# RWKV-7 mixer on Trainium2: key products leave PSUM by ScalarE copies and are masked in SBUF by GpSimd

## What is computed

```python
def rwkv7_scan(r, w, k, v, kk, a):
    def step(state, inp):
        r_t, w_t, k_t, v_t, kk_t, a_t = inp
        sa = jnp.einsum('...vk,...k->...v', state, kk_t)
        state = (state * w_t[..., None, :] - sa[..., :, None] * (kk_t * a_t)[..., None, :]
                 + v_t[..., :, None] * k_t[..., None, :])
        return state, jnp.einsum('...vk,...k->...v', state, r_t)
```

## Time and profile before

| | us |
|---|---|
| runs before, median of 3 | 5032.76 |
| lowest and highest of them | 5032.74, 5043.73 |
| the profiled execution, its own time | 5042.74 |
| its span, first to last instruction | 5041.1 |
| TensorE matmul busy in the span | 3743.1 (74%) |
| VectorE busy | 2186.9 (43%) |
| ScalarE busy | 1087.1 (22%) |
| GpSimd busy | 354.4 (7%) |
| the RWKV mixer, about | 872 to 1800 of the span |

### The profile page before, as it was taken

One profiled execution on the slowest core, in us unless ns is written; L12 is line 12 of the kernel. 1 busy time (PEld: TensorE's weight loads), 2 busy tenths in 40 slices (PEclk: granted clock), 3 DMA queues, 4 the chain that ended last, 5 costly groups with the idle time before them and its releaser, 6 DMA issues. The chain is left out here.

```text
span 5041.1 us, 52437 instructions
## 1 busy us (share of the span) xinstructions
PE 3743.1 (74%) x17350; PEld 2455.9 (49%) x17350; DVE 2186.9 (43%) x4798; ACT 1087.1 (22%) x2308; POOL 354.4 (7%) x437
## 2 busy tenths in 40 slices
PE   8699998677777868888466479923978856629980
PEld 1255554577667768888333234411446633314440
DVE  0212321666666646666378600053125525530007
ACT  0011222333333322222011112210124411102210
POOL 0000000211111100000000011110000000011001
PEclk9899999777777779999777689966989977859995
DMA  7622222300000011011523179953122251229984
GB/s 253 191 59 57 65 66 86 108 27 28 23 27 27 20 50 34 34 38 34 91 101 111 42 276 367 366 195 134 62 70 72 77 82 75 80 81 356 364 308 166
DMA packets 383411, 592.63 MB, mean 118 GB/s; under 512 B 61043, under 2 KB 266907, under 8 KB 383023
## 3 DMA queue, kind: packets, MB, share of 16 engines
q1 hardware_dynamic: 313934, 368.18, 23.9%
q10 hardware_dynamic: 47776, 151.99, 7.7%
q0 software_dynamic: 21584, 71.00, 4.3%
HBM read 466.29 MB, written 124.81 MB: 117 GB/s over the span
## 5 line engine op out<-in xcount | busy, mean ns | idle before, releaser
L373 PE MATMUL inp__bank<-inp__hT,inp__w 128*128 128x512 f32 (+1 forms) x1536 | 559.7, 524 | 10.1 <-DMA inp__w<-in_ab_w_in_dram 8.0
L2142 PE MATMUL moe__bank<-moe__wgu,moe__xT 128*128 128x512 f32 x1024 | 456.4, 599 | 13.2 <-DMA moe__wgu<-in_moe_w_up_dram 11.4
L373 PEld LDWEIGHTS inp__bank<-inp__hT,inp__w 128*128 128x128 f32 x1536 | 290.3, 191 | 272.1 <-issue 251.9
L1775 PE MATMUL close__bank<-close__w_out,close__catT 128*128 128x512 f32 x640 | 312.3, 650 | 101.3 <-DVEq L1916 93.9
L2142 PEld LDWEIGHTS moe__bank<-moe__wgu,moe__xT 128*128 128x128 f32 x1024 | 191.2, 192 | 233.9 <-issue 220.6
L1775 PEld LDWEIGHTS close__bank<-close__w_out,close__catT 128*128 128x128 f32 x640 | 132.5, 211 | 271.0 <-issue 186.4
L2265 DVE TENSOR_TENSOR moe__hid<-moe__sg,moe__bank 128x256 f32<-128x256 f32 x64 | 27.0, 421 | 480.2 <-ACT moe__sg L2204 480.2
L2159 PE MATMUL moe__bank<-moe__wdn,moe__hidT 128*128 128x512 f32 x512 | 230.5, 593 | 2.9 <-ACT moe__hidT L2208 2.9
L2460 PE MATMUL qkv__bank<-qkv__w,qkv__hT 128*128 128x512 f32 x480 | 212.1, 599 | 2.7 <-DVE qkv__hT L2552 2.7
L247 PE MATMUL ada__bank<-ada__w,ada__c_silu 128*2 128x512 f32 x384 | 170.5, 599 | 30.4 <-DMA ada__w<-in_ada_w_dram 27.9
L2035 POOL DMA_INDIRECT scratch_row_tok<-close__tok,close__dest_i x40 | 38.6, 965 | 2182.4 <-DVEq L1704 2170.8
(11 more groups left out here) (404 smaller groups left out, 6581.8 us busy)
## 6 DMA issues: line engine op xcount, KB each, us to landing
moe__wdn<-in_moe_w_down_dram ACTq DMA_DIRECT2D x64, 1024.0 KB, 8.6
moe__wgu<-in_moe_w_gate_dram SPq DMA_DIRECT2D x64, 1024.0 KB
moe__wgu<-in_moe_w_up_dram SPq DMA_DIRECT2D x64, 1024.0 KB
ada__w<-in_ada_w_dram SPq DMA_DIRECT2D x24, 2048.0 KB, 8.0
scratch_y_rows<-moe__y ACTq DMA_DIRECT2D x64, 512.0 KB
scratch_zt<-inp__tb SPq DMA_DIRECT2D x32, 640.0 KB, 5.0
inp__w<-in_ab_w_in_dram POOLq DMA_DIRECT2D x31, 512.0 KB, 4.6
delta__qkv<-scratch_zt SPq DMA_DIRECT2D x20, 768.0 KB, 4.4
```

Source lines behind the costliest of these rows:

```text
L373: mm = nc.tensor.matmul(zbank[j][g][:, 0:n], w[:, j, k, :], hT[:, k, t0:t0 + n], start=k == 0, stop=k == KC - 1)
L1775: mm = pe.matmul(bank[2 + c][:], catT[:, k, :], w_out[:, k, c * 512:(c + 1) * 512], start=k == 0, stop=k == KC - 1)
L2142: mm = pe.matmul(bank[2 + j][:], xT[:, j, k, :], wgu[:, j, k].rearrange("p a n -> p (a n)"), start=k == 0, stop=k == KC - 1)
```

## The change

The four BP instructions stay on VectorE. The four KP evictions leave it: ScalarE copies the four banks unmasked into KP (`copy_kp`), between `place(s+1)` and the eviction of `Un`, and GpSimd multiplies KP by the mask in place (`mask_kp`), between `key(s+3)` and `extra(s+3)`. Two semaphores are new, `kp_ev` (copied) and `kp_r` (masked). TensorE's waits for free banks go to `kp_ev`, and `from_state` waits for `kp_r`; GpSimd's `clear` waits for `kp_r` too, which its own queue has raised by then.

```diff
@@ tensor
                     if i > 0:
-                        pe.wait_ge(prod_ev, 8 * (i - 1) + 8)
+                        pe.wait_ge(kp_ev, 4 * i)
...
                     if have(i + 1):
-                        pe.wait_ge(prod_ev, 8 * (i + 1) + 8)
+                        pe.wait_ge(kp_ev, 4 * (i + 1) + 4)
...
                     if part == 0:
                         pe.wait_ge(hp, i + 1)
+                        pe.wait_ge(kp_r, 4 * i + 4)
@@ scalar
+                def copy_kp(i):
+
+                    if i > 1:
+                        act.wait_ge(pre_mm, i - 1)
+                    for q in (0, 2):
+                        for e in range(2):
+                            act.wait_ge(prod, 8 * i + (4 + q + e + 1))
+                            act.activation(KP[:, i % 2, e, q:q + 2].rearrange("p q a t -> p q (a t)"),
+                                           heads(bank[(6, 7, 2, 3)[2 * e + q // 2]][:], 256), ACT.Copy).then_inc(kp_ev, 1)
...
                     if have(s + 1):
                         place(s + 1)
+                    if have(s + 2):
+                        copy_kp(s + 2)
@@ gpsimd
+                def mask_kp(i):
+                    if i > 1:
+                        pool.wait_ge(x_clear, i - 1)
+                    for q in (0, 2):
+                        for e in range(2):
+                            pool.wait_ge(kp_ev, 4 * i + q + e + 1)
+                            pool.tensor_tensor(KP[:, i % 2, e, q:q + 2].rearrange("p q a t -> p q (a t)"),
+                                               KP[:, i % 2, e, q:q + 2].rearrange("p q a t -> p q (a t)"),
+                                               const(f"mask_k{i % 2}").unsqueeze(1).broadcast_to([P, 2, 256]), ALU.mult).then_inc(kp_r, 1)
...
                         key(s + 3)
+                    if have(s + 2):
+                        mask_kp(s + 2)
+                    if have(s + 3):
                         extra(s + 3)
@@ vector
                 def masked(i, d):
-                    for kind, mask in ((0, f"mask_b{d}"), (1, f"mask_k{d}")):
-                        if kind == 1 and i > 1:
-                            dve.wait_ge(pre_mm, i - 1)
...
+                    for q in (0, 2):
+                        for e in range(2):
+                                dve.wait_ge(prod, 8 * i + (q + e + 1))
+                                dve.tensor_tensor(BP[:, i % 3, e, q:q + 2].rearrange("p q a t -> p q (a t)"),
+                                                  heads(bank[2 + 2 * e + q // 2][:], 256),
+                                                  const(f"mask_b{d}").unsqueeze(1).broadcast_to([P, 2, 256]), ALU.mult).then_inc(prod_ev, 1)
```

More of the change, by code:

```diff
@@ L775, in rwkv_mixer @@
                                 "zeroed", "zero_stored", "rows_scaled"))
-        tr, tr_ev, prod, prod_ev, stacked, n_read, solved, d_placed, y5_mm, y5_ev, x64_mm, x64_ev, y6_mm, y6_ev, gt_mm, gt_ev, x_clear = (
-            ph.sem(n) for n in ("turned", "turned_ev", "products", "products_ev", "stacked", "lanes_read", "solved", "placed", "y5_mm",
+        tr, tr_ev, prod, prod_ev, kp_ev, kp_r, stacked, n_read, solved, d_placed, y5_mm, y5_ev, x64_mm, x64_ev, y6_mm, y6_ev, gt_mm, gt_ev, x_clear = (
+            ph.sem(n) for n in ("turned", "turned_ev", "products", "products_ev", "kp_copied", "kp_masked", "stacked", "lanes_read", "solved", "placed", "y5_mm",
                                 "y5_ev", "x64_mm", "x64_ev", "y6_mm", "y6_ev", "inverse_mm", "inverse_ev", "x_cleared"))
@@ L896, in products @@
                                 if kind == 1 and e == 1 and q % 2 == 0:
-                                    pe.wait_ge(prod_ev, 8 * i + (1 if q == 0 else 3))
+                                    pe.wait_ge(prod_ev, 4 * i + (1 if q == 0 else 3))
                                 b = bank[(2, 3, 4, 5, 6, 7, 2, 3)[4 * kind + 2 * e + q // 2]]
@@ L909, in level5 @@
                     if have(i + 1):
-                        pe.wait_ge(prod_ev, 8 * (i + 1) + 4)
+                        pe.wait_ge(prod_ev, 4 * (i + 1) + 4)
                     for e in range(2):
@@ L1050, in place @@
                         act.activation(XT[quad(b), j, :, quad(b)], solve.Q[quad(b)], ACT.Copy).then_inc(d_placed, 1)
+                def copy_kp(i):
[6 more added lines that the diff above has]
+                                           heads(bank[(6, 7, 2, 3)[2 * e + q // 2]][:], 256), ACT.Copy).then_inc(kp_ev, 1)
                 def stack(i):
-                    act.wait_ge(prod_ev, 8 * i + 4)
+                    act.wait_ge(prod_ev, 4 * i + 4)
                     if i > 0:
@@ L1180, in clear @@
                     pool.wait_ge(b_r, min(i + 3, NT))
+                    pool.wait_ge(kp_r, 4 * min(i + 2, NT))
                     pool.memset(X[quad(hi), i % 2, :, quad(lo)], 0.0).then_inc(x_clear, 1)
@@ L1224, in masked @@
                 def masked(i, d):
-                    for kind, mask in ((0, f"mask_b{d}"), (1, f"mask_k{d}")):
-                        if kind == 1 and i > 1:
-                            dve.wait_ge(pre_mm, i - 1)
-                        if kind == 0 and i > 2:
-                            dve.wait_ge(y_mm, i - 2)
-                            dve.wait_ge(y6_mm, i - 2)
-                        for q in (0, 2):
-                            for e in range(2):
-                                b = bank[(2, 3, 4, 5, 6, 7, 2, 3)[4 * kind + 2 * e + q // 2]]
-                                dst = (BP[:, i % 3, e, q:q + 2] if kind == 0 else KP[:, i % 2, e, q:q + 2])
-                                dve.wait_ge(prod, 8 * i + (4 * kind + q + e + 1))
-                                dve.tensor_tensor(dst.rearrange("p q a t -> p q (a t)"), heads(b[:], 256),
-                                                  const(mask).unsqueeze(1).broadcast_to([P, 2, 256]), ALU.mult).then_inc(prod_ev, 1)
+                    if i > 2:
+                        dve.wait_ge(y_mm, i - 2)
+                        dve.wait_ge(y6_mm, i - 2)
+                    for q in (0, 2):
[4 more added lines that the diff above has]
+                                                  const(f"mask_b{d}").unsqueeze(1).broadcast_to([P, 2, 256]), ALU.mult).then_inc(prod_ev, 1)
                 def state(i):
```

## The result

| | before | after |
|---|---|---|
| median of the runs, us | 5032.75 (5030.04 to 5043.73, 4 runs) | 5110.0 (5103.93 to 5116.93, 4 runs) |
| ratio, 95% interval | 1 | 1.015 (1.013 to 1.017) |
| profiled execution, us | 5042.74 | 5116.93 |
| its span, us | 5041.1 | 5115.2 |
| mean granted clock | 0.849 | 0.840 |

The kernel became 77 us slower. The time is inside the predicted range, but the sum of the prediction had only 47 of the 77 us. The table already says where the rest has to be looked for: of the 74.2 us between the two profiled executions 66.2 lie in the mixer and 11.6 in the closing stage, which the diff doesn't touch. All other stages together account for -3.6 us (DeltaNet 6.9 shorter, the others 3.3 longer).

A forecast was written before the change was run, and what follows sets the result against it. It took the mixer's chain through VectorE, from lane transposition to alpha, then TensorE as the bound. 46 us held plus 1.2 for first chunks, minus 0, gave +47 on 5032.76: 5080 us, range 5052 to 5122.

The forecast's parts named there:

- The bound of the step: Mixer step: VectorE's lane transposition waits for ScalarE's stack behind Un; its pause grows from 2.54 to about 5.0 us.
- KP evictions removed, gain 0: VectorE in the mixer: shedding four KP evictions, 2.47 us a chunk, is off the path and saves 0 us.
- the copies' cost: ScalarE ahead of Un: four KP copies fit its 3.02 us of idling, cost 0, with 0.6 us or more to spare.
- the 1.2 us for the first two chunks: First two chunks, without Un: the copies hold the stack and lane transposition by 0.6 us each, 1.2 us.
- VectorE held by GpSimd's masks, 2.3 us a chunk: Between lane transposition and alpha: masks hold VectorE instructions with two SBUF operands, 2.3 us over 20 chunks, 46 us.
- The first rival: Mixer: every mask costs VectorE a full turn, about 3.9 us a chunk, +78 us, 5111 us; chance 0.27.
- TensorE meanwhile idles and has slack: TensorE in the mixer: its 7.71 us wait for alpha becomes about 10, with no cost put on it.
- The spread of the steps: Mixer steps of 43.43 and 44.77 us with the same instructions: unassigned, between -14 and +7 us in all.
- if the step grows by something that isn't in VectorE's row: Mixer step: one of the signs by which the prediction said it would be wrong; no size given.
- No change: Mixer: masks don't hold VectorE, or the lateness is swallowed before alpha; +1.2 us, 5034 us; chance 0.08.
- faster: Mixer: VectorE's freed 2.47 us a chunk come off the path, 49 us, if the stack ends earlier; 4983 us; chance 0.03.
- late copies: ScalarE: copies of 0.9 us make Un slip about 0.6 us a step, 11 us more, 5091 us; chance 0.07.

The follow-up runs named there:

- stack_first: The kernel before with ScalarE's stacking of the BP blocks moved ahead of the eviction of Un: 4968.07 us, ratio 0.9882.
- idle_copies: The kernel before with four dummy ScalarE copies a chunk at the place of the KP copies, TensorE waiting for them: 5033.04 us against 5032.44, ratio 1.0001.
- idle_reads: The kernel before with four dummy GpSimd multiplications of 128x512 a chunk at the masks' place, on a spare tile: 5092.87 us against 5030.78, ratio 1.012.
- idle_writes: The kernel before with four GpSimd memsets of 128x1408 a chunk at the masks' place, writing only: 5030.34 us, ratio 1.000.
- warm_before: The kernel before with eight dummy matmuls a step in TensorE's wait for alpha: 4987.48 us, ratio 0.9912.
- warm_after: The changed kernel with ten dummy matmuls a step in TensorE's wait for alpha: 5051.7 us, ratio 1.0036 to before.
- late_pad: The changed kernel with masks behind the second rr, plus four tiny VectorE memsets a chunk where KP evictions were: 5033.18 us against 5030.61, ratio 1.0009.
- late_stack: The changed kernel with masks behind the second rr, the stack ahead of Un and the KP copies behind Un: 4985.32 us, ratio 0.9907 to before.
- late_mask: The changed kernel with GpSimd's masks behind the second rr of the next chunk instead of ahead of it: 5047.4 us against 5030.78, ratio 1.0031.

## Why the prediction was right or wrong

- **The bound of the step: right.** VectorE's pause ahead of the transposition was to be 5.0 us and is 4.93; stack_first shows from the other side that the stack bounds that arc.
- **KP evictions removed, gain 0: right**, and so is the copies' cost. ScalarE idles 0.82 us ahead of `Un`, inside the 0.6 to 1.4 foreseen; idle_copies measures 0. Of the 1.2 us for the first two chunks the trace shows the first 0.6: from the mixer's first matmul to the first lane transposition it is 20.7 us instead of 20.1.
- **VectorE held by GpSimd's masks, 2.3 us a chunk: right**, 2.25 in the trace, and the instructions named were the ones held, but for the 0.03 of H+Hp. The choice of who is held stood on two rows of before; idle_reads and idle_writes show that it is the reads. By the rule of the Trainium skill (SBUF — State Buffer, "Who interferes with whom") a VectorE instruction with two SBUF inputs is blocked by a GpSimd instruction that reads SBUF, and one with at most one such input (outside its two-port modes) isn't; the trace agrees on the reductions and the PSUM operand (0.57 and 0.69 us, unchanged) and the memsets' 0 us agrees on reading.
- **The first rival's 5111 us: right by accident.** It lies 1 us from the result, yet its mechanism isn't there. Either H+Hp was to take over 3 us, or the reductions and H<-bank were to be held. H+Hp takes 0.69 us, and they aren't. With the total alone I would have taken it for shown. The lengths of the single instructions say that it fell.
- **"TensorE meanwhile idles and has slack": this is the step that failed.** I read the 7.71 us of waiting as room. It is no work, but it has a price: the clock. The spread of the steps that I said I couldn't assign, 43.43 against 44.77 us, stood in the rows, and had I laid the granted clock beside them I would have found it. These are the windows of just these two steps of before (columns as above):

```profile
1281.40:1324.83 43.43, 33.06 (x242) 29.61 (x241) 28.97 (x63) 15.52 (x37) 7.68 (x7) 0.81 0.09 27
1324.83:1369.60 44.77, 35.35 (x242) 31.73 (x241) 28.97 (x63) 15.53 (x37) 7.68 (x7) 0.77 0.09 26
```

The same instructions, VectorE equally busy, TensorE busy 2.3 us longer at a lower mean clock: 16.1 us of the short step are at 1.2 GHz and 20.9 of the long one. The sum had 20 x 2.29 = 46 us for the held instructions, with 2.25 measured, and nothing for TensorE. The mixer grew by 66.2, so some 21 us come on top, 1.15 us in each of the steps of the table. warm_before and warm_after take 0.95 of these 1.15 us away. The prediction had put -14 to +7 us for it, as chance and not as a cost that follows from the lateness.
- **A stage that isn't in the diff: missed, 11.6 us.** The prediction named "if the step grows by something that isn't in VectorE's row" as its mistake, and looked no further than the step. late_pad shows that it goes with the 80 instructions fewer on VectorE; why their number matters stays open.
- **No change, faster, late copies: not borne out.** "Faster" was to need something that ends the stack earlier. With the stack ahead of `Un`, 62 us come from that alone, and freeing VectorE on top of it (late_stack) gave no more.

The account: 45 us held, 21 from the clock, 11.6 from the closing stage, together 78 against 77 measured in the runs. The terms come from one profile each, the first is a middle step taken twenty times (instruction by instruction it is 43, and the clock's part then 23), and -3.6 us of other stages are left out, so an agreement within 1 us is luck. As a second account, idle_reads has the first two without the third, and costs 62 us. That 5110 us lay inside the range was luck in part, too: the forecast was 5080, and it was for the first rival, whose mechanism isn't there, that the range reached up to 5122.

## What to carry to other kernels

Put GpSimd work that reads SBUF where VectorE waits or reads PSUM, not by how idle GpSimd is: the same masks a few instructions later in its order cost the mixer nothing, where the early ones cost it 66 us. Before moving work off an engine that waits, ask what it waits for: two lines on ScalarE, the stack ahead of an eviction that was less urgent, gave 62 us. An idle TensorE isn't free, so price each us of lateness ahead of it above one us where rows show its clock falling (here 2.25 us cost 3.40), and judge a change also in the stages that it doesn't touch.

## What the runs showed of the hardware that I had not expected

- VectorE and GpSimd took turns even in a run of four GpSimd operations: the four masks took 6.19 us in after, where VectorE's held instructions got in between (1.26, 1.72, 1.72 and 1.60 us), and 4.97 us in late_stack, where VectorE stands idle beside them:

```profile
1299.95 4.97 POOL L1195 TENSOR_TENSOR rwkv__KP<-rwkv__KP,rwkv__consts 128x512 f32<-128x512 f32 x4
```

- A GpSimd memset of 1.26 us holds no VectorE instruction (692 and 575 ns, as ever), in 80 of them.
- A later alpha costs more than its own lateness, through TensorE's clock: 2.25 us of lateness became a step longer by 3.40, while with dummy matmuls 2.26 became 2.46.
- 80 instructions fewer on VectorE in the mixer brought 21 packets of code instead of 6 into a stage some 700 us later, and 11.6 us. The packets are 0.17 MB in all; VectorE's waits of 3.27 us are where the stage gets longer, and one packet starts in each of the three in late_mask.
